# Products that nobody reads, placed in TensorE's waits ahead of the attention output, in the routing and around the last expert

## What is computed

```python
o = rmsnorm(concat(outs), subln) * (1.0 - lambda_init)   # differential attention, 8 heads of 128
x = x + o.reshape(B, T, H * 2 * dh) @ w_out
xt = rmsnorm(x, norm_ffn)
logit_g = xt @ w_group + b_group                         # 4 groups
logit_e = (xt @ w_router + b_router)                     # 4 experts in each group
g_sel = argmax(logit_g);  top_v, top_i = top_k(softmax(logit_e[g_sel]), 2)
combine = one_hot(g_sel) * (top-2 weights, normalised) * softmax(logit_g)[g_sel]
y = sum over experts e: combine[e] * (silu(xt @ w_gate[e]) * (xt @ w_up[e])) @ w_down[e]
x = x + y
```

## Time and profile before

| | us |
|---|---|
| three timed runs | 1574.33, 1577.47, 1578.65 |
| median | 1577.47 |
| the profiled execution, its own time | 1572.86 |
| its span, the stretch that the profile covers | 1571.0 |
| TensorE busy | 1505.6 (96%) |
| VectorE, ScalarE busy | 779.9, 674.1 |
| mean granted clock of TensorE | 0.979 of full speed |

### The profile page before, as it was taken

One profiled execution on the slowest core, in us unless ns is written; L12 is line 12 of the kernel. 1 busy time (PEld: TensorE's weight loads), 2 busy tenths in 40 slices (PEclk: granted clock), 3 DMA queues, 4 the chain that ended last, 5 costly groups with the idle time before them and its releaser, 6 DMA issues.

```text
span 1571.0 us, 19018 instructions
## 1 busy us (share of the span) xinstructions
PE 1505.6 (96%) x7399; PEld 1245.2 (79%) x7399; DVE 779.9 (50%) x941; ACT 674.1 (43%) x853; POOL 78.9 (5%) x57
## 2 busy tenths in 40 slices
PE   8899999999899999999999999999889789999996
PEld 8888888888787788888888887788557678888874
DVE  6433323232566335232332216335773679898884
ACT  5322222212355424222222124433772368777773
POOL 0000000000000000000000000000130012111210
PEclk9999999999999999999999999999998889999998
DMA  6123222232230032322223232232131379999993
GB/s 242 60 101 107 82 105 92 96 107 94 81 108 28 8 114 81 107 83 103 100 87 108 92 109 81 98 107 81 57 140 76 144 276 383 384 394 395 382 381 87
DMA packets 36207, 226.18 MB, mean 144 GB/s; under 512 B 5271, under 2 KB 5527, under 8 KB 11824
## 3 DMA queue, kind: packets, MB, share of 16 engines
q1 hardware_dynamic: 31392, 212.06, 35.9%
q0 software_dynamic: 4608, 13.22, 3.6%
q10 hardware_dynamic: 144, 0.03, 0.0%
HBM read 215.22 MB, written 13.63 MB: 146 GB/s over the span
## 4 chain that ended last, share of the span: by engine, by line
PE 53%; DVE 5%; DMA 3%; ACT 2%; issue 2%; DVEq 0%; ACTq 0%; SPq 0%; POOLq 0%
PE PS L255 16%; PE PS L257 16%; PE PS L256 16%; DMA eraw<-experts 3%; PE PS L1642 1%; PE PS L1662 1%; ACT WEH L2399 1%; PE PS L2332 1%; PE PS L1653 1%; DVE da_flat L1716 1%; DVE WL L250 1%; DVE WEL L2461 1%; PE PS L1982 1%; PE PS L1453 0%; PE PS L2355 0%
## 5 line engine op out<-in xcount | busy, mean ns | idle before, releaser
L250 DVE TENSOR_TENSOR WL<-raw,WH 128x2048 fp32r<-128x2048 f32 x93 | 214.0, 2301 | 432.8 <-ACT WH L245 432.8
L255 PE MATMUL PS<-AH,WL 128*128 128x512 f32 (+1 forms) x768 | 286.7, 373 | 4.3 <-DVE AL L303 4.3
L256 PE MATMUL PS<-AL,WH 128*128 128x512 f32 (+1 forms) x768 | 286.0, 372 | 0.0
L257 PE MATMUL PS<-AH,WH 128*128 128x512 f32 (+1 forms) x768 | 285.9, 372 | 0.0
L245 ACT ACTIVATE WH<-raw 128x2048 fp32r<-128x2048 f32 x93 | 177.6, 1910 | 241.2 <-PE PS L257 241.2
L2461 DVE TENSOR_TENSOR WEL<-eraw,WEH 128x2048 fp32r<-128x2048 f32 x96 | 217.3, 2287 | 21.7 <-ACT WEH L2399 21.4
L2399 ACT ACTIVATE WEH<-eraw 128x2048 fp32r<-128x2048 f32 x96 | 182.4, 1915 | 35.1 <-DMA eraw<-experts 24.5
L255 PEld LDWEIGHTS PS<-AH,WL 128*128 128x128 f32 x768 | 145.6, 190 | 29.7 <-DVE AL L303 4.5
L257 PEld LDWEIGHTS PS<-AH,WH 128*128 128x128 f32 x768 | 145.5, 189 | 25.0
L256 PEld LDWEIGHTS PS<-AL,WH 128*128 128x128 f32 x768 | 145.6, 190 | 24.8
L255 PE MATMUL PS<-WH,AL 128*128 128x512 f32 (+2 forms) x416 | 156.3, 376 | 7.7 <-DVE WL L250 7.7
(11 more groups left out here) (317 smaller groups left out, 2112.7 us busy)
## 6 DMA issues: line engine op xcount, KB each, us to landing
eraw<-experts SPq DMA_DIRECT2D x96, 1024.0 KB, 15.6
raw<-stream SPq DMA_DIRECT2D x94, 1024.0 KB, 4.8
out<-X SPq DMA_DIRECT2D x5, 512.0 KB, 2.7
moe_rows<-moe_rows_g SPq DMA_DIRECT2D x5, 512.0 KB, 2.7
X<-x SPq DMA_DIRECT2D x4, 512.0 KB, 5.4
ffn_row<-rows SPq DMA_DIRECT2D x2, 512.0 KB, 9.2
final_row<-rows SPq DMA_DIRECT2D x2, 512.0 KB, 5.9
cst<-consts SPq DMA_DIRECT2D x1, 739.5 KB, 13.6
```

The source lines that it names most:

```text
L250: dve.tensor_tensor(WL[:, u % SLOTS, :], raw[:, u % SLOTS, :], WH[:, u % SLOTS, :].bitcast(F32), ALU.subtract).then_inc(unit_lo, 1)
L255: pe.matmul(acc, lhs_lo, rhs_hi, start=start, stop=False)
L256: pe.matmul(acc, lhs_hi, rhs_lo, start=False, stop=False)
L257: return pe.matmul(acc, lhs_hi, rhs_hi, start=False, stop=stop)
```

## The change

A helper issues n products of 128 x 128 by 128 x 512 into one bank, each starting its own sum, and nothing reads them. Their operands are the high half of an output unit that is in its slot already (ahead of the attention output) or chunk 3 of `AL` (elsewhere). Ten groups of them are placed ahead of waits of TensorE. The first place also gets a wait for the unit that the fillers read. Nothing else changes.

```diff
+        def keep_busy(pe, bank, n, some=None):
+
+            some = AL[:, 3, :] if some is None else some
+            for _ in range(n):
+                pe.matmul(PS[:, bank, :], some[:, 0:P], some[:, 0:512], start=True, stop=True)
...
             @block.tensor
             def _(pe):
+                pe.wait_ge(unit_lo, u0 + 1)
                 for t in range(T):
+                    keep_busy(pe, 2 * t, (20, 0, 6, 5)[t], WH[:, u0 % SLOTS, :])
                     pe.wait_ge(normal, t + 1)
                     for c in range(C):
                         mm = pe.transpose(PS[:, 2 * t + c // 4, (c % 4) * P:(c % 4 + 1) * P],
...
                 table(0)
-
+                keep_busy(pe, 0, 5)
                 pe.wait_ge(selected, 3)
...
                 mm.then_inc(ranked, 1)
+                keep_busy(pe, 0, 9)
                 table(1).then_inc(tabled, 1)
-
+                keep_busy(pe, 0, 12)
                 pe.wait_ge(weighted_out, 1)
...
                 mm.then_inc(shares_tabled, 1)
+                keep_busy(pe, 0, 6)
...
                     turn_rows(0)
+                    keep_busy(pe, 0, 8)
                     gate(0, 0)
                     gate(0, 1)
                     turn_rows(1)
...
                             gate(n + 1, 0)
+                        if n == E - 1:
+                            keep_busy(pe, 3, 8)
                         turn_h(n)
+                        if n == E - 1:
+                            keep_busy(pe, 3, 5)
                         if n + 1 < E:
                             gate(n + 1, 1)
```

## The result

The changed kernel takes 1570.76 us (median of 16 runs, 1565.54 to 1575.13) against 1576.28 for the kernel before (16 runs, 1571.04 to 1581.22): a ratio of 0.9967, 95% interval 0.9953 to 0.9981, so 5.5 us less. The forecast was 1570.9, 6.5 us under the median then known.

A forecast was written before the change was run, and what follows sets the result against it. TensorE's clock was taken to halve after short waits and narrow matmuls, so real work is paid at half speed. Terms -1.85 - 1.95 - 2.75 = -6.55 us from the median 1577.47 gave 1570.9 us, range 1565.5 to 1576.5.

The forecast's parts named there:

- Ahead of the attention output: Fillers of 20, 6 and 5 fit their waits, transposes run at full clock, first output product earlier: gain 1.85 us.
- The first two groups in the routing: The 5 run at half clock, 1.1 us late; the clock returns inside the 9, with no further delay.
- Tables: In the routing, at full clock the second table gains 0.4 us and the share table 1.85 us.
- The gate: First expert's 24 gate products: 1.7 us to win at full clock, half of it taken, -0.8 us.
- Routing and gate together: Sum of the routing's delay, both tables and the first gate: -1.95 us, bounds -5.7 to +4.2.
- Rival 1: The clock holds in the routing too: -10.3 us in all, 1567.2 us; chance 0.14.
- The experts move with their gate: In the expert stage, the dense transfer stretch begins a fixed time after the first gate and moves with it.
- rival 3: Transfers set the end of the experts whatever comes before; only the tail gains, -2.75 us, 1574.7 us; chance 0.07.
- The tail: Around the last expert, fillers of 8 and 5 fit; transposes -0.45, last products -2.35: gain 2.75 us, between 2.3 and 2.9.
- The base: Gains were subtracted from the timed median, 1577.47 us, not from the profiled execution, 1572.86 us, which lay 4.6 us below.
- The slower rival: Fillers paid at half clock ahead of the attention output and in the routing: +3.9 us, 1581.3 us; chance 0.06.
- the rule: Transpose mode on TensorE does not count as busy the same way and does not engage the full clock.

The follow-up runs named there:

- change_again: The changed kernel unaltered, profiled a second time; its one run took 1566.04 us.
- route_only: The change with only its fillers in the routing and ahead of the first gate; 1573.46 us, ratio 0.9997 to the kernel before.
- in_waits: The change without 5 and 9 in the routing, with 3 between the last tile's transposes and 16 instead of 8 ahead of the first gate; 1565.49 us.
- out_20_only: The change without the groups of 6 and 5 ahead of the attention output, the 20 kept; its one run took 1572.92 us.
- among_logits: The change with eight more fillers among the 20-column matmuls of the second pair; 1568.63 us, ratio 0.9958 to the kernel before.
- hold_all: The change with eight more fillers among the second pair's 20-column matmuls and 20 instead of 8 ahead of the first gate; 1570.29 us, ratio 0.9958.
- gate_38: The change with 38 instead of 8 fillers ahead of the first gate; 1576.75 us.

## Why the prediction was right, point by point

- **Ahead of the attention output: right.** -1.85 forecast, -1.60 measured, the same in nine other profiles with the three groups. Tile 2's transposes came 0.88 us sooner (0.95 forecast), the last eight and what follows took 0.74 less (0.9 forecast).
- **The first two groups in the routing: half right.** The fall in the narrow matmuls and the 5 fillers at half clock, 1.1 us late, came as forecast: the ranks began 2.97 us behind the logits instead of 1.91. The step that failed is "So the clock returns inside the 9 fillers: ... no further delay". In the change's profile it returned at 1257.2, 13.7 us after the fall, and the second table was 1.1 us later still. I had taken the stretches that brought the clock back, two rows of pure products, as the pattern of a stretch that is a mixture of fillers and narrow matmuls. Even where it did return inside the 9 (change_again), at about the eighth of them, these made the table 0.8 us later than the 5 had. In the seven profiles with both groups and a low clock it returned inside the 9 three times, always near their end, and C was never under 11.7.
- **Tables: right in kind, small in size.** Second table to share table -0.17 (forecast -0.4), share table to gate -1.68 (forecast -1.85). The share table's 2.00 us were forecast as 1.85.
- **The gate: under-rated in this profile.** -1.55 against a forecast of -0.8, which was half of what can be had. With 8 fillers the clock held in four profiles and was lost in four (7.1 to 7.2 us), so half was a fair mean. But in two of the four that held (change_again, route_only) only 1.4 us were left idle, because the clock had fallen a second time and the fillers took longer. With 3.0 us idle it held in two of six, with 1.2 to 1.4 in all three, in_waits among them.
- **Routing and gate together:** 1.1 + 1.1 - 0.2 - 1.7 - 1.55 = -1.2 against -1.95. Up to the share table the change came out 1.3 us worse than forecast (+2.0 against +0.7), in the gate 0.75 better; that the one makes up for half of the other is luck.
- **Rival 1's condition:** it had the clock hold if the fall came late enough to meet fillers. In out_20_only the fall came 4.3 us behind the first 20-column matmul, inside the 5, and in change_again 3.7 us behind it, 0.4 us ahead of them. The clock was low afterwards both times. Only among_logits, with fillers between the narrow matmuls, held it, and hold_all with the same ones did not.
- **The experts move with their gate: right** as far as one profile of gate_38 shows; F under rival 3, 272 to 273 us, lies below every profile on record.
- **The tail: right.** Transposes and what follows 2.12 us instead of 2.49 (-0.37, forecast -0.45), products 5.72 instead of 7.86 (-2.14, forecast -2.35), together -2.5 against -2.75. The base of this term is one profile; against the tail of route_only the same fillers win 1.6 us, less than the lower bound of 2.3. The fall before lies at 1549.7 by its window (0.86), not at 1549.9; nothing rests on that.
- **The base.** That this profile of before lay 4.6 us under the median was left unexplained. Part of it is now seen: it is one of the four profiles in which the clock held throughout the attention, worth 1.5 to 3 us against the others. Subtracting from the median of timed runs was the better choice. Over more runs that median came down by 1.2 us to 1576.28, which with a gain 1 us smaller than forecast left the forecast time almost met: 1570.76 against 1570.9 is closer than the terms deserve.

The slower rival was made of the rule that the prediction quotes from the Trainium skill (TensorE: Matmul & The Clock Gate, Part 4: PE-mode transpose). It did not come: the clock held through all of the attention output in every profile with the three groups. But fillers stood beside the transposes each time, so these runs don't test the rule alone. The kernel before is the better test, and the prediction read it too weakly: by the window of 0.54 the clock came back at about 1187.92, and the first product started at 1187.93, so since the fall TensorE had completed nothing but transposes. route_only shows the same again. Here the return came behind transposes alone, against the rule.

## What to carry to other kernels

Filling a wait of TensorE pays where the clock is known to be full when the filler starts and the work behind the wait is on the path: 20, 6 and 5 products in waits of that size won 1.6 us in every profile, and 8 and 5 won 2.5 us against the tail of before or 1.6 against that of route_only. Count fillers at the half-clock price wherever the clock may have fallen before them, and leave out those that do not fit at that price; here two groups made a chain of short alternating steps 0.5 to 1.9 us longer. A group placed just ahead of real work can bring the clock back itself, as the 12 did here three times, and little idle time should be left between it and that work: the gate kept the full clock each time behind 1.2 to 1.4 us, and two times in six behind 3.0.

## What was not expected of the hardware

- The clock can stay at 0.50 for 13.7 us while TensorE is busy throughout: so it was in the change from 1243.5 to 1257.2, with matmuls of 20, 48 and 64 columns, the 5 and 9 fillers and the first three of the 12. In the three profiles without 5 and 9 it came back inside the row of 12 fillers, with 2.57 us of idle time and a narrow table ahead of them.
- After a return it can soon be lost again: in change_again, route_only and hold_all it fell a second time behind the share table, 6.8 us after it had come back.
- The same program loses its clock in different places. Up to the end of the differential attention the thirteen profiled executions run the same instructions, and no filler stands there; yet in the attention the clock held in four of them, fell once in five and twice in four, at 1.5 us for each fall. This and the 3.5 us of spread in the expert stage are together as large as the whole change, which is why stretches of one trace say more than its end.
